# Moving the split tokens: one tile with spare room, a start of its own for each norm

## The reference, cut to what matters

```
x = x + 0.5 * swiglu(rms_norm(x, ffn1_norm[l]), w1, w3, w2)     # norm 3l
h = rms_norm(x, mix_norm[l]); z = h @ w_in[l]                    # norm 3l + 1
...  neighbourhood attention, gated linear attention, latent attention on slices of z
x = x + mixed @ w_out[l]
x = x + 0.5 * swiglu(rms_norm(x, ffn2_norm[l]), w1, w3, w2)     # norm 3l + 2
```

## Time and profile before

| what | value |
|---|---|
| median of 3 runs | 1665.01 us (1664.18 to 1665.88) |
| span of the profiled execution | 1662.6 us |
| TensorE matmuls | busy 1611.2 us, 97% of the span, 11156 instructions |
| weight loads | busy 1454.2 us, 87% |
| VectorE | busy 1065.9 us, 64% |
| ScalarE | busy 825.5 us, 50% |
| GpSimd | busy 264.3 us, 16% |
| chain that ended last | TensorE 83%, VectorE 11%, ScalarE 2% |

### The profile page before, as it was taken

One profiled execution on the slowest core, in us unless ns is written; L12 is line 12 of the kernel. 1 busy time (PEld: TensorE's weight loads), 2 busy tenths in 40 slices (PEclk: granted clock), 3 DMA queues, 4 the chain that ended last, 5 costly groups with the idle time before them and its releaser, 6 DMA issues.

```text
span 1662.6 us, 27116 instructions
## 1 busy us (share of the span) xinstructions
PE 1611.2 (97%) x11156; PEld 1454.2 (87%) x11156; DVE 1065.9 (64%) x1269; ACT 825.5 (50%) x1123; POOL 264.3 (16%) x208
## 2 busy tenths in 40 slices
PE   7999999999999999999999999999999999999997
PEld 7999888888989998999988888999999887879885
DVE  4655557665765455555565766566555679867985
ACT  5443446653454433543454665335443556655563
POOL 0000060010000000000034000000000069306940
PEclk9999999999999999999999999999999999999999
DMA  7757555333546655555746444255565455155612
GB/s 226 224 183 232 176 179 167 121 127 102 173 157 203 200 178 177 181 187 191 231 158 195 127 145 128 102 178 169 186 200 178 135 185 194 33 157 165 218 33 89
DMA packets 206612, 273.97 MB, mean 165 GB/s; under 512 B 18774, under 2 KB 167096, under 8 KB 206008
## 3 DMA queue, kind: packets, MB, share of 16 engines
q1 hardware_dynamic: 206376, 272.67, 51.2%
q10 hardware_dynamic: 144, 0.00, 0.0%
HBM read 271.61 MB, written 1.08 MB: 164 GB/s over the span
## 4 chain that ended last, share of the span: by engine, by line
PE 83%; DVE 11%; ACT 2%; issue 2%; POOL 1%; DMA 0%; SPq 0%; POOLq 0%; ACTq 0%; DVEq 0%
PE bank L503 29%; PE bank L550 14%; PE bank L985 8%; PE bank L974 7%; PE bank L1175 4%; DVE wlo L435 2%; PE bank L2037 2%; PE bank L2286 2%; PE bank L1257 2%; PE bank L2015 1%; PE bank L1118 1%; PE bank L956 1%; PE bank L1093 1%; ACT whi L424 1%; PE bank L2122 1%
## 5 line engine op out<-in xcount | busy, mean ns | idle before, releaser
L435 DVE TENSOR_TENSOR wlo<-raw,whi 128x2048 fp32r<-128x2048 f32 (+1 forms) x258 | 584.0, 2268 | 335.6 <-ACT whi L424 335.0
L424 ACT ACTIVATE whi<-raw 128x2048 fp32r<-128x2048 f32 (+1 forms) x258 | 484.1, 1880 | 319.6 <-PE bank L550 101.4
L503 PE MATMUL bank<-hT_hi,whi 128*128 128x256 f32 x1408 | 395.7, 281 | 0.8 <-DVE hT_lo L354 0.3
L503 PE MATMUL bank<-hT_lo,whi 128*128 128x256 f32 x1408 | 394.2, 280 | 0.0
L503 PE MATMUL bank<-hT_hi,wlo 128*128 128x256 f32 x1408 | 394.1, 280 | 0.0
L503 PEld LDWEIGHTS bank<-hT_hi,whi 128*128 128x128 f32 x1408 | 266.3, 189 | 3.5 <-issue 0.9
L503 PEld LDWEIGHTS bank<-hT_lo,whi 128*128 128x128 f32 x1408 | 266.4, 189 | 1.4
L503 PEld LDWEIGHTS bank<-hT_hi,wlo 128*128 128x128 f32 x1408 | 266.3, 189 | 0.0
L550 PE MATMUL bank<-whi,Y 128*128 128x512 f32 x704 | 223.9, 390 | 0.0
L308 POOL TENSOR_TENSOR st<-st 128x1 f32<-128x1 f32 x18 | 17.6, 980 | 938.8 <-ACT X L301 938.8
L550 PEld LDWEIGHTS bank<-whi,Y 128*128 128x128 f32 x704 | 132.2, 188 | 26.8
(11 more groups left out here) (396 smaller groups left out, 2822.6 us busy)
## 6 DMA issues: line engine op xcount, KB each, us to landing
raw<-in_ffn_w SPq DMA_DIRECT2D x132, 1024.0 KB, 5.5
raw<-in_w_in SPq DMA_DIRECT2D x80, 1024.0 KB, 5.5
raw<-in_w_out SPq DMA_DIRECT2D x16, 1024.0 KB, 4.9
raw<-in_w_br_na SPq DMA_DIRECT2D x4, 1024.0 KB, 6.0
raw<-in_w_br_mla SPq DMA_DIRECT2D x4, 1024.0 KB, 5.1
raw<-in_w_br_gla SPq DMA_DIRECT2D x4, 1024.0 KB, 5.0
raw<-in_cmp_k_w SPq DMA_DIRECT2D x4, 1024.0 KB, 6.4
raw<-in_cmp_v_w SPq DMA_DIRECT2D x4, 1024.0 KB, 5.2
```

Source lines behind the costliest of these rows:

```text
L424: act.activation(m["whi"][:, slot, 0:w], m["raw"][:, slot, 0:w], ACT.Copy).then_inc(s.hi_ready, 1)
L435: dve.tensor_tensor(m["wlo"][:, slot, 0:w], m["raw"][:, slot, 0:w], m["whi"][:, slot, 0:w].bitcast(F32), ALU.subtract).then_inc(s.lo_ready, 1)
L503: mm = pe.matmul(B[bank][:, mt * T:(mt + 1) * T], a, b, start=(n == 0 and k == 0), stop=(n == KK - 1 and k == 2))
```

## The change

The two tiles of the tokens become one tile, `hsplit`, with both halves behind one another and room for 88 elements (352 bytes) more. Each norm's tokens begin at a place of their own, `HT_PLACE[n]` elements above the tile's start, where `hT_hi` lay before. The places are 64, 192, 192, 256, 224, 224, 320 and 96 bytes for norms 0 to 7. All that is allocated behind (`KEEP`, `consts`, `st`, `par`, `ident_r`, `mask_r`) lies 352 bytes higher. No instruction, wait, shape or transfer is added or taken away.

```diff
+HT_PLACE = (16, 48, 48, 64, 56, 56, 80, 24)
...
-        hT_hi = sb("hT_hi", [P, KK, T], F32R)
-        hT_lo = sb("hT_lo", [P, KK, T], F32R)
+        hsplit = sb("hsplit", [P, 2 * KK * T + 88], F32R)
...
-        hT = lambda kk, a=0, n=T: (hT_hi[:, kk, a:a + n], hT_lo[:, kk, a:a + n])
+
+        def tokens(n):
+            whole = hsplit[:, HT_PLACE[n]:HT_PLACE[n] + 2 * KK * T].rearrange("p (i k t) -> p i k t", i=2, k=KK)
+            return lambda kk, a=0, n=T: (whole[:, 0, kk, a:a + n], whole[:, 1, kk, a:a + n])
+
...
-        act.activation(m["hT_hi"][:, kk, t * P:(t + 1) * P], self.xT(banks, kk, t), ACT.Copy,
+        act.activation(m["tokens"](n)(kk, t * P, P)[0], self.xT(banks, kk, t), ACT.Copy,
                        scale=gain[:, kk:kk + 1]).then_inc(s.hThi_ready, 1)
...
-        dve.scalar_tensor_tensor(m["hT_lo"][:, kk, t * P:(t + 1) * P], self.xT(banks, kk, t),
-                                 gain[:, kk:kk + 1], m["hT_hi"][:, kk, t * P:(t + 1) * P].bitcast(F32), ALU.mult,
+        hi, lo = m["tokens"](n)(kk, t * P, P)
+        dve.scalar_tensor_tensor(lo, self.xT(banks, kk, t),
+                                 gain[:, kk:kk + 1], hi.bitcast(F32), ALU.mult,
                                  ALU.subtract).then_inc(s.hT_ready, 1)
...
+        self.hT = m["tokens"](norm)
...
-                    for k, (a, b) in enumerate(passes(w, self.m["hT"](kk))):
+                    for k, (a, b) in enumerate(passes(w, self.hT(kk))):
...
+    hT = m["tokens"](n0 + 1)
...
+    hT = m["tokens"](n0)
```

More of the change, by code:

```diff
@@ L363, in act_high_both @@
             act.wait_ge(s.hT_ready, 2 * K_ORDER.index(kk - 1) + 2)
-        act.activation(m["hT_hi"][:, kk, :], m["B"][banks[kk // 2]][:, (kk % 2) * T:(kk % 2 + 1) * T], ACT.Copy,
+        act.activation(m["tokens"](0)(kk)[0], m["B"][banks[kk // 2]][:, (kk % 2) * T:(kk % 2 + 1) * T], ACT.Copy,
                        scale=gain[:, kk:kk + 1]).then_inc(s.hThi_ready, 2)
@@ L369, in dve_low_both @@
         dve.wait_ge(s.hThi_ready, 2 * i + 2)
-        dve.scalar_tensor_tensor(m["hT_lo"][:, kk, :], m["B"][banks[kk // 2]][:, (kk % 2) * T:(kk % 2 + 1) * T],
-                                 gain[:, kk:kk + 1], m["hT_hi"][:, kk, :].bitcast(F32), ALU.mult,
+        hi, lo = m["tokens"](0)(kk)
+        dve.scalar_tensor_tensor(lo, m["B"][banks[kk // 2]][:, (kk % 2) * T:(kk % 2 + 1) * T],
+                                 gain[:, kk:kk + 1], hi.bitcast(F32), ALU.mult,
                                  ALU.subtract).then_inc(s.hT_ready, 2)
@@ L790, in first_layer @@
     unit = lambda step: UM + MIX_FIRST[step]
-    par, st, X, G, Y, KEEP, B, C, x, hT = (m[k] for k in ("par", "st", "X", "G", "Y", "KEEP", "B", "C", "x", "hT"))
+    par, st, X, G, Y, KEEP, B, C, x = (m[k] for k in ("par", "st", "X", "G", "Y", "KEEP", "B", "C", "x"))
+    hT = m["tokens"](n0 + 1)
     gain = [par[:, 8 * n:8 * n + 8] for n in range(3)]
```

## The result

The changed kernel takes 1675.01 us (median of 4 runs, 1674.7 to 1677.73) against 1664.65 us of the kernel before on the same chip: a ratio of 1.0068, 95% interval 1.0054 to 1.0082. It is slower by 0.7%; 1650 us had been forecast.

The account below looks back on a forecast made before the run. TensorE's matmul spacing was taken to bound the kernel; 7.2 + 1.9 + 0.6 + 5.0 = 14.7 us off 1662.6 gives 1647.9, plus 2.4 for the median, 1650 us. Range 1634 to 1674 us.

Parts of the forecast that it names:

- What bounds the kernel: Whole kernel: TensorE's matmuls, busy 97% of the span; in the feed-forward a faster matmul shortens the time one for one.
- Tokens moving: Lines 503, 985, 2037: 5712 matmuls that count drop 1.7 ns to 115.0, gaining 7.2, 1.9 and 0.6 us.
- the slower rival: Line 503 falls to line 1175's 120.2 ns as reads meet mid-matmul; 1680 to 1685 us, chance 0.20.
- Two shares in the sum: Parts of matmuls taken as on the chain: 0.4 for line 2037, half of line 2015's count.
- The reading of the two pairs: Lines 503/1175 and 550/974: same shape, 116.7 against 120.2 and 227.5 against 233.3 ns, so the start address matters.
- Tokens stationary: Lines 974, 956, 1257 and 2015: 864 matmuls that count go from 233.3 to 227.5 ns, gaining 5.0 us.
- The starts at a multiple of 64 bytes: Comparing line 503's pieces in norms 5 and 4 with 0, 2 and 3 tells whether such starts matter; no size.
- What must stay: Lines 550 (557 after; 24 in 5.46 us), 1175 (120.2 ns), 2190 (113.3 ns) stay, else it is not the distance.
- The skill's rule: TensorE's two read ports are independent and it never waits, so the sum would be nothing: 1665 us.

## Why the prediction was wrong

**What bounds the kernel** was right. A matmul's spacing is the currency: norm by norm the longer pieces add up to the result. In the loops 11 x (0.32 + 0.16 + 0 + 0.31) = 8.7 us for the gate and up products. Line 993 costs about 0.9 us at norm 1 and 1.9 at norm 4 (672 x 0.85 matmuls by 1.6 and 3.3 ns), line 2046 about 0.9 at norms 6 and 7. The stationary tokens give back 384 x 6.7 ns = 2.6 us at norm 4, and line 557, at 5.49 for 5.46, takes 0.7 in norms 0 and 2. That is 10.5 us; the span grew by 10.7.

**The failed step is "Tokens moving".** It took 115.0 ns, the middle between line 2190's 113.3 and the present 116.7. Neither row is of this shape at another distance. The measured paces at the new distances are these, from pieces of 96 and 144 in the chain (norm 7's, distance 20's and the second values from the starts within a stream). Two values in a field are two steady paces that were seen at that distance:

| distance | 256 tokens moving, ns | 512 weight columns moving, ns |
|---|---|---|
| 0 (norms 4, 5, and `Y`) | 119.9 | 226.7 |
| 4 | 118.6 or 116.7 | 233.3 or 226.7 |
| 8 (before, norm 3) | 116.7 or 117.8 | 233.3 |
| 10 | 119.7 | |
| 12 | 118.4 | |
| 16 | 117.8 or 113.3 | 233.3 |
| 20 | 118.3 or 120.0 | 232.1 |
| 24 (norms 0, 6) | 120.0 | 234.2 |
| 32 (norm 7) | 118.7 | 232.1 |
| 40 | 118.6 | 233.3 |
| 48 | 117.8 or 113.3 | 228.9 |
| 56 (norms 1, 2) | 118.3 | 233.3 |
| 60 | 117.2 | 226.7 or 228.4 |

The old distance had the lowest pace that the loops ever showed with `Y` at 0, and seven of the eight norms left it for one at 118.3 ns or more (6 and 7 count for little). The mean over the 5712 matmuls that count was about 118.8 ns, where the slower rival had 120.2 and called 118.1 the point from which the loss can be measured. So the rival called slower had the direction, at 60% of its price (2.1 of 3.5 ns). That the two reads meet in the middle of a matmul, as it put it, no run shows; the run with fewer weight columns shows only that the stationary side has a part in it.

Two shares in the sum are loose and did no harm: 2% of the span against line 2037's 101 us is 0.33 and not 0.4, and 1% against 45 us is 0.37 and not a half. The chain's own list has 2.4% and 1.4% there, which give 0.40 and 0.52.

**The reading of the two pairs** was half right. The start matters, and the pairs' opposite order is real: distance 0 is bad for 256 columns and good for 512. But the distance was counted modulo 512 bytes, where norm 3's 288 and norms 4 and 5's 256 looked new. Modulo 256 norm 3 stood where it had always been, and 4 and 5 stood where `Y` was, at line 1175's pace, so this row could have priced them. The period was not to be read from the trace of before: all its long streams have distance 0 or 8. What it did offer was the row of the very same spacing, and it was set aside for a middle value.

**"Tokens stationary"** took 5.0 us for every norm but got 2.6, from norm 4 alone. "A distance 32 bytes short of equal is the only slow one seen" turned a sample of two into a rule; in the table the fast ones are the exception (0, 60, 48 and once 4).

**The starts at a multiple of 64 bytes** mean nothing in themselves: moving everything by 32 bytes changed nothing.

**What must stay** stayed for line 1175 (119.9 ns) and line 2190 (113.3 ns), but line 557's 24 went from 5.46 to 5.49 us after the streams at 24 and 56. That is the first sign of what the later runs showed plainly: a stream's pace depends on more than its own distance.

**The skill's rule.** The runs show a pace that depends on where the moving and the stationary operand start relative to one another, 120.0 against 116.7 ns, and on the number of weight columns, 120.0 against 117.5 ns. The Trainium skill, "SBUF — State Buffer", section "Who interferes with whom", has TensorE's two read ports independent; by that this change would have cost nothing. The measurement decides against it here. At the lower clock the excess is gone, 0.21 us for 256 columns.

**What stays open** is why some distances cost more than others, what picks one of two paces at a stream's entry, and why the loops are fast with `Y` at 48 and not at 16. In the runs the loops were fast in the one kernel with tokens and `Y` both at 48, and a pace changed only behind other instructions or a wait; none of them shows the mechanism. Distances 20 and 32 were seen in the second block's streams alone; 28, 36, 44 and 52 were not tried.

## What to carry to other kernels

When streams of one shape differ in spacing and no wait explains it, compare where the moving and the stationary operand start, modulo 256 bytes here, before touching anything else. With `Y` where it was, no new place made the loops faster, and most made them slower, so a sweep of one table is worth more than an argument from two rows. Price an unseen distance by the whole range of the rows of its own shape (here 116.7 to 120.2 ns), not by the best row of another shape; even a distance two elements from a known one was off by 3 ns. Choose the places of all operands that follow one another in a loop together: here each moved alone gained nothing, and both together, with the tiles that moved along, gained 0.9%.

## What the runs showed of the hardware

- The spacing of matmuls with 256 fp32r columns moving and 128 stationary lies between 113.3 and 120.0 ns at the upper clock, by the distance of the operands and by what ran before. With 512 columns it lies between 226.7 and 234.2 ns, in another order of distances.
- The pace repeats with 256 bytes (16 and 80 elements: 11.31 us for 96; 0 and 64: 11.51).
- One distance can have two steady paces (48 and 16: 113.3 and 117.8 ns; 8: 116.7 and 117.8 ns). The same stream can have the one in one layer and the other in the next, and keeps it for up to 167 matmuls.
- The granted clock of the second block's first layer was 0.98 in the kernel before (170.7 us) and 0.96 in the one with all places zero (173.7 us) and in the one with both at 48 (173.6 us), so a difference of 3 us in that stretch, between single executions, says nothing about the change.
